# One section for the recurrence matrices and the four inverses of a transformer block, on one core

## The reference

```python
def step(S, inp):                      # RWKV-7, per head, 512 times
    r_t, w_t, k_t, v_t, a_t, b_t = inp
    sa = einsum('bhij,bhj->bhi', S, a_t)
    S = S * w_t + outer(sa, b_t) + outer(v_t, k_t)
    return S, einsum('bhij,bhj->bhi', S, r_t)

def block(qi, i):                      # differential attention, 128 queries
    s = where(mask, einsum('bqhcd,bkhcd->bhcqk', qi, kh) * scale, -inf)
    p = softmax(s)
    return einsum('bhqk,bkhe->bqhe', p[:, :, 0] - lam * p[:, :, 1], vh)
```

## Time and profile before

| What | Value |
|---|---|
| median of 3 runs | 3473.29 us (3472.57 to 3474.38) |
| span of the profiled execution | 3469.9 us |
| median less that span | 3.4 us |
| mean granted clock of TensorE | 0.950 |
| busy: PE, DVE, ACT, POOL | 93%, 50%, 35%, 5% |
| first matmul of the eight stages | 592.99 us |
| first transposition after them (L986) | 819.35 us |

### The profile page before, as it was taken

How to read it: one execution, slowest core, us unless ns; L and a number is a source line. 1 busy time by engine, 2 the same in 40 slices (tenths; PEclk the granted TensorE clock), 3 DMA queues, 4 the chain that set the end, 5 groups by cost and what they waited for, 6 DMA issues and landing times. The chain is left out here.

```text
span 3469.9 us, 42364 instructions
## 1 busy us (share of the span) xinstructions
PE 3241.5 (93%) x17616; PEld 2562.8 (74%) x17616; DVE 1750.0 (50%) x2596; ACT 1207.3 (35%) x1725; POOL 181.0 (5%) x178
## 2 busy tenths in 40 slices
PE   8999998898799998999999999998998899899998
PEld 6888776677578886877557788876777788678885
DVE  4446536554544455767875433325763234543434
ACT  4333342223433333333334322223663223342323
POOL 0000000211000000000000000001203410000000
PEclk9999998778899999999999999999998899999999
DMA  3225321000222353222003222231221001122322
GB/s 135 97 97 201 133 82 55 2 2 8 85 85 97 116 207 134 92 90 73 1 1 110 79 97 97 98 103 50 79 79 57 25 32 55 63 90 97 97 97 91
DMA packets 76367, 285.19 MB, mean 82 GB/s; under 512 B 8464, under 2 KB 8592, under 8 KB 75152
## 3 DMA queue, kind: packets, MB, share of 16 engines
q1 hardware_dynamic: 76176, 282.47, 24.2%
HBM read 276.15 MB, written 6.29 MB: 81 GB/s over the span
## 5 line engine op out<-in xcount | busy, mean ns | idle before, releaser
L149 DVE TENSOR_TENSOR wlo<-raw,whi 128x1024 fp32r<-128x1024 f32 x450 | 554.2, 1232 | 1242.0 <-ACT whi L144 1241.8
L144 ACT ACTIVATE whi<-raw 128x1024 fp32r<-128x1024 f32 x450 | 476.3, 1059 | 1192.8 <-PE ps L173 1189.2
L171 PE MATMUL ps<-h_hi,wlo 128*128 128x512 f32 x1800 | 724.9, 403 | 44.7 <-DVE wlo L149 12.0
L172 PE MATMUL ps<-h_lo,whi 128*128 128x512 f32 x1800 | 707.4, 393 | 0.0
L173 PE MATMUL ps<-h_hi,whi 128*128 128x512 f32 x1800 | 707.4, 393 | 0.0
L171 PEld LDWEIGHTS ps<-h_hi,wlo 128*128 128x128 f32 x1800 | 341.6, 190 | 134.5 <-issue 48.3
L172 PEld LDWEIGHTS ps<-h_lo,whi 128*128 128x128 f32 x1800 | 341.9, 190 | 74.1 <-issue 6.0
L173 PEld LDWEIGHTS ps<-h_hi,whi 128*128 128x128 f32 x1800 | 341.5, 190 | 72.7
L171 PE MATMUL ps<-mid_hi,wlo 128*128 128x512 f32 x784 | 307.4, 392 | 0.0
L173 PE MATMUL ps<-mid_hi,whi 128*128 128x512 f32 x784 | 305.0, 389 | 0.0
L172 PE MATMUL ps<-mid_lo,whi 128*128 128x512 f32 x784 | 305.0, 389 | 0.0
(11 more groups left out here) (573 smaller groups left out, 4674.6 us busy)
## 6 DMA issues: line engine op xcount, KB each, us to landing
raw<-in_wstream SPq DMA_DIRECT2D x453, 512.0 KB, 3.5
mod_ring<-in_wmod SPq DMA_DIRECT2D x48, 512.0 KB, 4.6
c_rows<-in_c_rows SPq DMA_DIRECT2D x3, 1024.0 KB, 5.7
x<-in_x_t SPq DMA_DIRECT2D x4, 512.0 KB, 7.7
x_saved<-x SPq DMA_DIRECT2D x1, 2048.0 KB, 9.0
x<-x_saved SPq DMA_DIRECT2D x1, 2048.0 KB, 8.1
mix_saved_d<-x SPq DMA_DIRECT2D x1, 2048.0 KB, 8.2
out<-x SPq DMA_DIRECT2D x8, 256.0 KB, 2.1
```

What stands on the lines that cost most here:

```text
L144: act.activation(k.whi[:, n % SPLIT, :], k.raw[:, n % RAW, :], ACT.Copy).then_inc(k.hi_ready, 1)
L149: dve.tensor_tensor(k.wlo[:, n % SPLIT, :], k.raw[:, n % RAW, :], k.whi[:, n % SPLIT, :].bitcast(F32), ALU.subtract).then_inc(k.split_read ...
L171: pe.matmul(out, wlo, hi, start=first, stop=False)
L172: pe.matmul(out, whi, lo, start=False, stop=False)
```

## The change

One function replaces the eight stages. The 32 jobs of the four pairs run through in one block; eleven steps of the inverse of pair c-1 (level 0, then two for each level) are dealt out between the eight jobs of pair c by the list `beside`, before (half 0) and after (half 1) the value products; the fourth inverse follows behind the last job. The 34 attention steps are dealt out as 10 in the first eight jobs, 5 in each further eight, and 9 beside the fourth inverse. The value products go into the same bank as the products of their job, so products n+1 now wait for ACT's copies of job n-1, and value products n wait for the last mask of job n. Of `at` and `arb` only the diagonal blocks are computed, by four matmuls of 64 columns in place of two of 128, and masked by one instruction each. `at` has two buffers. The mask table grows by one matrix, `halves`. `Inverses` has the instructions of `invert`, with `act`, `dve` and `gp` beside the `pe` shown. POOL's program is the four inverses in a row.

```diff
-        "eye", "fold0", "fold1", "fold2", "swap", "count"]
+        "eye", "fold0", "fold1", "fold2", "swap", "count", "halves"]
...
+class Inverses:
+    PAIRS, LEVELS = 4, 6
+    STEPS = 2 * LEVELS - 1
...
+        self.x, self.t, self.m = ([tmp[:, 2 * i + g, :] for g in range(2)] for i in range(3))
+        self.tx, self.out = ([k.ps[:, 2 + g, 256 * i:256 * i + 256] for g in range(2)] for i in range(2))
...
+    def gp(self, gp, c):
...
+        for l in range(self.LEVELS):
+            for g in range(2):
+                if l == 0:
+                    gp.wait_ge(self.at_ready, 8 * c + 4 * g + 4)
...
+                else:
+                    gp.wait_ge(self.t_done, self.twelve(c, l - 1, g))
...
+    def pe(self, pe, c, step):
+        k, l = self.k, (step + 1) // 2
+        for g in range(2):
...
+            if step == 0:
...
+            elif step % 2:
+                pe.wait_ge(self.masked, self.twelve(c, l, g))
+                pe.wait_ge(self.x_added, self.added(c, l - 1, g))
...
+                for o, r in self.BLOCKS:
+                    mm = pe.matmul(tx[o, r], m[o, r], x[o, r], start=True, stop=True)
+                mm.then_inc(self.t_done, 1)
+            else:
+                pe.wait_ge(self.t_copied, self.ten(c, l, g))
...
+                for o, r in self.BLOCKS:
+                    if l < self.LEVELS - 1:
+                        pe.matmul(tx[o, r], xt[o, r], t[o, r], start=True, stop=True)
+                    mm = pe.matmul(out[o, r], t[o, r], xt[o, r], start=True, stop=True)
+                mm.then_inc(self.x_done, 1)
...
-def rwkv_matrices(k, c, rw, a_t, b_t, v_tok, at, arb, rv, y, bg, slices):
+def rwkv_matrices_and_inverses(k, rw, a_t, b_t, v_tok, tri, arb, rv, y, xt, tmp, diff):
...
-    jobs = [(q, T) for q in range(2) for T in range(TT)]
-    names = ("mats_ready", "am_ready", "at_ready", "arb_ready", "v_ready", "kept")
-    with stage(k.nc, *names) as (block, mats_ready, am_ready, at_ready, arb_ready, v_ready, kept):
-        gaps = bg.gaps(*slices * 4)
+    jobs = [(c, q, T) for c in range(4) for q in range(2) for T in range(TT)]
+    last = len(jobs)
...
+        beside = ((0,), (1,), (), (2,), (3,), (), (4,), (5,), (), (6,), (7,), (), (8,), (9,), (10,), ())
+        begin, middle, end = (1, 1, 1, 2, 1, 1, 1, 2), (1, 0, 1, 0, 1, 1, 0, 1), (1, 1, 1, 1, 1, 0, 1, 1, 1, 0, 1)
+        gaps = diff.gaps(*begin, *middle * 3, *end)
+
+        def steps(n, half):
+            return [] if n < 8 else beside[2 * (n % 8) + half]
 
         def products(pe, n):
...
             if n >= 2:
-                pe.wait_ge(arb_ready, 2 * (n - 1))
-            for m, (left, right) in enumerate(((key, a_t), (key, r), (b_t, a_t), (b_t, r))):
-                mm = pe.matmul(ps[:, m * P:m * P + P], left[hp, c, tk], right[hp, c, tk],
-                               start=True, stop=True)
+                pe.wait_ge(kept, 2 * (n - 1))
+            for m, right in enumerate((a_t, r)):
+                pe.matmul(ps[:, m * P:m * P + P], key[hp, c, tk], right[hp, c, tk], start=True, stop=True)
+            for m, right in enumerate((a_t, r)):
+                for b in range(2):
+                    o, tb = slice(64 * b, 64 * b + 64), slice(T * P + 64 * b, T * P + 64 * b + 64)
+                    mm = pe.matmul(ps[o, 2 * P + 64 * m:2 * P + 64 * m + 64], b_t[hp, c, tb], right[hp, c, tb],
+                                   start=True, stop=True)
...
             products(pe, 0)
-            for n, (q, T) in enumerate(jobs):
-                if n + 1 < 8:
+            for n, (c, q, T) in enumerate(jobs):
+                if n + 1 < last:
                     products(pe, n + 1)
-                bg.pe(pe, gaps[n])
+                for step in steps(n, 0):
+                    inv.pe(pe, c - 1, step)
+                diff.pe(pe, gaps[n])
...
-                pe.wait_ge(am_ready, n + 1)
-                if n >= 2:
-                    pe.wait_ge(kept, 2 * (n - 1))
-                pe.matmul(k.ps[:, 2 + n % 2, 0:64], am[:, n % 2, 0:P], v_tok[:, T, hc],
-                          start=True, stop=True)
-                pe.matmul(k.ps[hp, 2 + n % 2, P:2 * P], v_tok[:, T, hc], am[:, n % 2, P:2 * P],
+                pe.wait_ge(arb_ready, n + 1)
+                pe.matmul(k.ps[:, n % 2, 0:64], am[:, n % 2, 0:P], v_tok[:, T, hc], start=True, stop=True)
+                pe.matmul(k.ps[hp, n % 2, 64:64 + P], v_tok[:, T, hc], am[:, n % 2, P:2 * P],
                           start=True, stop=True).then_inc(v_ready, 1)
+                for step in steps(n, 1):
+                    inv.pe(pe, c - 1, step)
+            for step in range(inv.STEPS):
+                inv.pe(pe, 3, step)
+                diff.pe(pe, gaps[last + step])
...
         def _(dve):
...
-                for b in range(2):
-                    o = slice(64 * b, 64 * b + 64)
-                    dve.tensor_tensor(at[o, q, 64 * T:64 * T + 64], ps[o, 2 * P + 64 * b:2 * P + 64 * b + 64],
-                                      k.mats[o, MAT["strict"], o], ALU.mult).then_inc(at_ready, 1)
-                    dve.tensor_tensor(arb[o, 2 * c + q, T, :], ps[o, 3 * P + 64 * b:3 * P + 64 * b + 64],
-                                      k.mats[o, MAT["incl"], o], ALU.mult).then_inc(arb_ready, 1)
-                bg.dve(dve, gaps[n])
...
+                dve.tensor_tensor(tri[c % 2][:, q, 64 * T:64 * T + 64], ps[:, 2 * P:2 * P + 64], halves[:, 0:64],
+                                  ALU.mult).then_inc(at_ready, 1)
+                dve.tensor_tensor(arb[:, 2 * c + q, T, :], ps[:, 2 * P + 64:3 * P], halves[:, 64:P],
+                                  ALU.mult).then_inc(arb_ready, 1)
+                for step in steps(n, 0):
+                    inv.dve(dve, c - 1, step)
+                diff.dve(dve, gaps[n])
+                for step in steps(n, 1):
+                    inv.dve(dve, c - 1, step)
...
         def _(act):
...
-                bg.act(act, gaps[n])
+                for step in steps(n, 0):
+                    inv.act(act, c - 1, step)
+                diff.act(act, gaps[n])
                 act.wait_ge(v_ready, n + 1)
...
-    tri, tmp = at(k, "at", 54, [P, 2, 256]), at(k, "inverse_tmp", 56, [P, 6, 256])
+    tri, tmp = [at(k, "at", kb, [P, 2, 256]) for kb in (54, 138)], at(k, "inverse_tmp", 56, [P, 6, 256])
...
-        for c in range(4):
-            rwkv_matrices(k, c, rw, a_t, b_t, v_tok, tri, arb, rv, y, diff, (1, 0))
-            invert(k, [tri[:, g, :] for g in range(2)],
-                   [xt[:, 2 * c + g, :, :].rearrange("p a n -> p (a n)") for g in range(2)], tmp, diff, (1, 0))
+        rwkv_matrices_and_inverses(k, rw, a_t, b_t, v_tok, tri, arb, rv, y, xt, tmp, diff)
...
+    m["halves"] = np.concatenate([a < b, a <= b], 1)
```

More of the change, by code:

```diff
@@ L1297, in _, with __init__, twelve, ten @@
                 bg.dve(dve, gaps[3 + c])
-def rwkv_matrices(k, c, rw, a_t, b_t, v_tok, at, arb, rv, y, bg, slices):
+class Inverses:
+    PAIRS, LEVELS = 4, 6
+    STEPS = 2 * LEVELS - 1
+    BLOCKS = [(slice(64 * b, 64 * b + 64), slice(64 * p, 64 * p + 64)) for p in range(PAIRS) for b in range(2)]
+    def __init__(self, k, at, xt, tmp, at_ready, sems):
+        self.k, self.at, self.xt, self.at_ready = k, at, xt, at_ready
+        (self.masked, self.t_done, self.t_copied, self.x_done, self.x_added, self.xt_added, self.xt_begun) = sems
+        self.x, self.t, self.m = ([tmp[:, 2 * i + g, :] for g in range(2)] for i in range(3))
+        self.tx, self.out = ([k.ps[:, 2 + g, 256 * i:256 * i + 256] for g in range(2)] for i in range(2))
+    def twelve(self, c, l, g):
+        return 12 * c + 2 * l + g + 1
+    def ten(self, c, l, g):
+        return 10 * c + 2 * l + g - 1
+    def added(self, c, l, g):
+        return 10 * c + 2 * l + g + 1
+    def split(self, ap):
+        return ap.rearrange("p (a n) -> p a n", a=self.PAIRS)
+    def gp(self, gp, c):
+        k, split = self.k, self.split
+        eye = k.mats[:, MAT["eye"], 0:64]
+        for l in range(self.LEVELS):
+            for g in range(2):
+                if l == 0:
+                    gp.wait_ge(self.at_ready, 8 * c + 4 * g + 4)
+                    if c:
+                        gp.wait_ge(self.t_done, self.twelve(c - 1, self.LEVELS - 1, g))
+                else:
+                    gp.wait_ge(self.t_done, self.twelve(c, l - 1, g))
+                if l == 1:
+                    gp.wait_ge(self.xt_begun, 2 * c + g + 1)
+                gp.tensor_tensor(split(self.m[g]), split(self.at(c, g)), bcast_mid(fold(k, l), self.PAIRS), ALU.mult)\
+                  .then_inc(self.masked, 1)
+                if l == 0:
+                    gp.wait_ge(self.masked, self.twelve(c, 0, g))
+                    gp.tensor_tensor(split(self.xt(c, g)), split(self.m[g]), bcast_mid(eye, self.PAIRS), ALU.add)\
+                      .then_inc(self.xt_begun, 1)
+    def pe(self, pe, c, step):
+        k, l = self.k, (step + 1) // 2
+        for g in range(2):
```

(98 more changed lines are left out.)

6 lines of the change are left out of this document (4 added, 2 removed).

## The result

The change makes the kernel a little slower. Its median is 3489.14 us in 12 executions (3472.53 to 3496.18), beside 3474.14 us for the kernel before on the same chip: a ratio of 1.0037 [1.0024, 1.005]. I had forecast 3461 us.

What follows compares the result with a forecast made beforehand. PE, half of the time at half clock, was taken to bound the eight stages. First eight jobs 50, middle 129 and fourth inverse 35 made 214 us against 226.4, 12 us less: 3473.3 - 12 = 3461 us, range 3440 to 3500.

Steps and rivals of the forecast that it cites:

- nothing else of the program moves: Outside the eight replaced stages (226.4 us, 6.5% of the span), the scan behind them included, no time was expected to change.
- rival (1): Middle of the section stays at half clock: 185 us in place of 129, time 3517; in part or whole, chance 0.20.
- First eight jobs 50: Jobs without an inverse beside them, at half clock: 23 us of jobs, 13 of attention, 13.5 of waits, sum 50.
- The middle 129: Other 24 jobs with three inverses at full clock: sum 123, plus five clock drops of 1.2 us each, 128 or 129.
- my 13 us for PE's part of the attention: In the first eight jobs: five even attention steps, twice 1.25 us each, and 4.2 us of head-closing products, put at 13.
- Waits for the copies: Products wait for ACT's copies of job n-1, behind attention exponentials: 13.5 us in first eight jobs, 14.3 and 2.3 in middle.
- A job's products: Four 64-column products replacing two of 128 save 0.15 us a job at full clock, 0.35 at half.
- Steps that wait for others: Sign of being wrong: steps waiting for POOL, ACT or DVE by more than 5 us in sum.
- The even split: By the skill's rule alone the middle would run half and half between clock levels: 157 us, time 3489.
- Rival (2): Wait for the copies twice as long because DVE is late: up to 17 us more in the middle, 3478; chance 0.15.
- (4): Attention's chain through DVE and ACT bound the stretch all along, so PE's new order changes nothing; with unseen causes, chance 0.05.
- (3): Fuller gain: no clock drops in the middle, first eight jobs 37 us at full clock; up to 22 us better, 3440; chance 0.15.

Runs made afterwards that it cites:

- the filler: One extra 256-column matmul ahead of the wait in each scan turn but the first: changed kernel 3461.28 us; kernel before 3472.58; changed kernel with copies reordered too 3433.85.
- two delay matmuls: Kernel before with two unused matmuls (512 and 128 columns) ahead of the transpositions between section and scan: 3491.57 us, ratio 1.0059.
- the usual execution: Changed kernel run again unedited and profiled in an execution of 3489.68 us; median 3486.86 us in 8, ratio 1.0034 to the kernel before.
- four delay matmuls: Changed kernel with four unused 512-column matmuls ahead of the transpositions between section and scan: 3491.39 us, ratio 1.0056.
- copies first: Changed kernel with ACT's two copies of a job ahead of the attention step's exponentials, except at jobs 3 and 7: 3452.09 us, ratio 0.9949.

## Why the prediction was wrong

**The step that failed** is the half sentence in which I took the stretch out of the program: "nothing else of the program moves". I had the scan's rows before me and read its 1.00 as a property of small matmuls with waits. It was one outcome of two. The change moved the scan by 15 us, it fell to 0.50 after 27.3 us, and 17.9 us went. That this is the clock and nothing handed over is shown by the filler; that the scan is as fragile in the kernel before, by its two delay matmuls, which cost it the same. In the terms of my sum, everything behind the section stood at nothing, and the scan alone measured 17.9 us more, 17.6 in the usual execution, in which it was moved by only 2 us and lost the clock all the same. I had used the scan as evidence against rival (1), and should have asked what else leans on the clock right behind the edited stretch.

**Point by point**, in the profiled execution of 3472.53 us:
- Section 214 us: 210.4. First eight jobs 50: 50.1, at 0.52. The middle 129: 124.5, at 0.89, with 27 us at 0.50 where my five drops make 15. Fourth inverse 35: 35.8.
- In the first eight jobs my 13 us for PE's part of the attention don't follow from the parts I give, five times twice 1.25 and 4.2, which make 16.7 and a sum of 53. The timeline has 13.1 (9.1 and 4.0), so the total was right and its parts were not.
- Waits for the copies 13.5 + 14.3 + 2.3 = 30 us by my parts: 28.4, at 20 jobs (10.6 in the first eight, 17.8 in the middle). The barriers' 10 us came back.
- A job's products 0.15 us shorter at full clock and 0.35 at half: 0.06 and 0.24, so 3.4 us over the 32 jobs in place of 6.4. A new mask 217 ns: 215 and 216. The run of these two alone shows that even this saving need not reach the time.
- Steps that wait for others: 3.5 us (the ACT copy behind the exponentials, for which I had put 3) and 1.6, all in the fourth inverse, and 1.2 of an attention step. That is 5.1 to 6.3 in sum and over the 5 that I had named as a sign of being wrong; but my sum had 5.5 for the fourth inverse itself, so the sign was set too tight.

**The median** has a second cause. In the usual execution the middle runs at 0.78 and takes 137.6 us. This is under the 0.85 that I had named as the sign of rival (1), which came true in small part: 8.6 us over my 129, of the 56 that it would cost in whole. A section of 223.6 us gains only 2.8. The Trainium skill has the swing between the two levels in TensorE: Matmul & The Clock Gate, section A second HAM failure mode: psum-queue depth-cycling; this middle, in which PE waits for a bank at 13 of 24 jobs, does swing, though more than half of its time is at the full level in both profiles (0.89 and 0.78). The even split that I put on it, for which the page gives no share, came to 3489 us, the median that came out. That is a coincidence: it put the whole loss into the middle (157 us against the 124.5 and 137.6 seen), while most of it came in the scan.

Rival (2) is out: the waits are as long as taken, not twice. So is (4): with ACT's order changed, the same attention chain lets the section finish in 186 us. (3), the fuller gain, was not reached by the change.

## What to carry to other kernels

When an edit shortens a stretch, look for stages behind it that are sparse on TensorE, and ask what each costs at half clock: here 18 us, more than the edit gained. Here a filler matmul per turn (2.8 us) held the full clock in all three profiles that have it, and with it in both kernels the change measured 11.3 us better in place of 15 worse. And where a producer's bank waits for a small copy, put that copy ahead of the long work in the copying engine's queue: this order gave 24 us of the section in the profiled executions.

## What the hardware showed that I had not expected

- The identical instructions of the scan, some 616 recorded matmuls, took 49.6, 55.8 or 64 to 68 us in nine profiles of kernels without the filler. The kernel before lost the clock with its scan 23.8 us behind the last rise in place of 22.8, and the changed one kept it at 12.8 in place of 10.2.
- In five profiles (the changed kernel's two, four delay matmuls, copies first, and the kernel before with its delay) the clock fell 27.3 to 27.7 us after the scan's start, and the rest of the scan ran at 0.50. With PE counted busy for 25.6 of those 27.3 us, the count doesn't show that a fall is coming.
- Small matmuls in a row of waits can spend more or less of their time at 0.50 with no change in the code between two executions: 61 of 137.6 us and 27 of 124.5 us for the same middle. The kernel before has levels of its own: of its 25 executions in one comparison seven lay at 3462 to 3465 us, seventeen at 3472 to 3475 and one at 3488.
